# Attention values with the probabilities moving: v beside 64 columns of ones as the stationary side, gates in turned form, a new order of steps

## The chip, the cores and the metric

One Trainium2 chip, one of its cores. The metric is device time in microseconds (us). The kernel before takes 269.6 us (median of 3 runs, 269.55 to 269.61). A change of less than 0.2% can't be told from none with this kernel.

## What is computed

Two layers on x (256 positions by 1024 channels, float32), each with an RMS norm ahead of it, a residual add behind it, and a final RMS norm. The part that matters here, cut from the reference:

```python
z = hn @ w_in                                    # even: 1024 x 3584, odd: 1024 x 4096
u, v, g_a, q, k, vv, g_b = jnp.split(z, cuts)    # even layer
y_a = chunked_gmlp(u, v, ...) * silu(g_a)        # 4 groups of 128 channels, chunks of 128
y_b = moba_attention(q, k, vv) * silu(g_b)       # 8 heads of 64; one block of 256: causal softmax
h = h + concat([y_a, y_b]) @ w_out
q, k, v, g = jnp.split(hn @ w_in, 4)             # odd layer, 16 heads of 64
y = dilated_mixture(q, k, v)                     # three windows merged by their denominators
h = h + (y * silu(g)) @ w_out
```

With 256 positions both attentions are an ordinary causal softmax under one additive mask: for each head scores, exp, row sums, and y = (P v) / rowsum. SiLU is taken as g/2 times (1 + tanh(g/2)).

## The kernel before

**Products.** Every weight matrix is multiplied in three parts, so that float32 precision comes out of a cheaper form: w is split into `w_hi` (rounded to fp32r by ACT, L605) and `w_lo` (the rest, a subtraction on DVE, L743), and the activations into `hnT_hi`/`hnT_lo` or `yT_hi`/`yT_lo`; a product is hi·hi + lo·hi + hi·lo. The weights stream through `w_raw` (3 slots of 4 x 128 rows by 512 columns, loaded by SyncE) and are split by quarter (2 x 128 rows) into 9 slots.

An output of 512 columns is a *group*; a group takes two of four PSUM banks (`pair(group)`). A group consists of *items* (a quarter of weights each), an item of two half-items, and a half-item is what PE does between two other steps. There are two forms. In the **plain** form (values, gMLP inputs, gates, output projections; L1003 to L1005) 128 positions are the stationary side and 512 weight columns move: two tiles x three parts = 6 matmuls in a half-item (3 where it is for one tile: output projections and odd values). In the **turned** form (queries and keys; L962, L964, L966) 128 weight columns are stationary and 256 positions move: 12 matmuls in a half-item, and the result has channels on partitions.

**Attention of a head.** PE: `scores` (L1022, L1023) into a score bank. DVE: mask, scale and row minimum (L876). ACT: exp, with the row sums in `den` by `accum_out` (L655). PE: `transpose` (3 turns, L914) of the probabilities. ACT: copy to `probsT` (L663). For a pair of heads PE then does `values`: turned probabilities stationary (128 x 128), 64 columns of v moving, three float32 matmuls a head (L1045 to L1047), each of which is two records of the trace. DVE: reciprocal of four row sums and one multiply into `y` (L883, L885). The y of 8 heads is multiplied by its gate (`gating`, L859, L863), and every 256 channels of y are turned by PE again (`y_pair`, 4 turns, L914), rounded by ACT (L667) and split by DVE (L893) for the output projection.

**Order.** `steps()` writes one list that every engine walks, doing its own part of each step and waiting on semaphores. The list is the product half-items in order, with the other steps put in by tables: `HEADS_AT` (for each set of 8 heads the half-items at which values, transposes and scores stand), `EVEN_AT`, `NORM_AT`, `ODD_AT`, `END_AT`; `LAST_ROUND` bounds how far the splits of weights run ahead. Engines are in-order: what is written later in the list waits behind what is written earlier on the same engine. In the even layer the groups are vv, k, q, v, gb (gate of the attention), u, ga, then the output projection; in the odd layer two tiles of v, q, k, q, k, two gates, and the output projection. A product waits on `lo_ready` for its quarter, an output product also on `y_lo`; a `values` step waits on `attended` of the pair before it, since there is one `value_bank`. Below, "half-item n" counts product half-items from the start, 0 to 199: gb is 32 to 39, u 40 to 47, ga 48 to 55, the even output projection starts at 56, the second odd q is 136 to 143, the odd gates 152 to 167, the odd output projection starts at 168.

## Time and profile before

| | |
|---|---|
| median of 3 runs | 269.6 us |
| the profiled execution, its own time | 269.5 us |
| its span, first to last instruction | 267.7 us |
| PE busy (matmul) | 259.2 us, 97% |
| PE weight loads, beside the matmuls | 230.9 us, 86% |
| DVE busy | 179.2 us, 67% |
| ACT busy | 158.7 us, 59% |
| POOL busy | 24.2 us, 9% |
| mean granted TensorE clock | 0.994 |

The duration of one matmul in the trace is from its start to the modelled end of its results, and the next one begins long before that: the cost of a matmul in a stream is the distance from its start to the next start, not its duration. The same holds to a smaller degree for DVE and ACT, where a start follows the one before by some 0.06 to 0.09 us less than its duration. Where rows are merged ("x3") the second column is the time from the first start to the last end.

### The profile page before, as it was taken

To read this page: it belongs to the slowest core of one execution; us is meant where nothing else is said; L and a number is where in the kernel's file an instruction comes from. 1 tells how busy PE (TensorE), PEld (TensorE's weight loads), DVE (VectorE), ACT (ScalarE), POOL (GpSimd) and SP (SyncE) were. 2 spreads that over 40 slices of the span, in tenths; PEclk is the share of its full clock that TensorE was granted. 3 is DMA by queue.
4 is the path that set the end of the run, shared out by engine and by line. 5 is a ranking of instruction groups with operands and counts; after the bars stand their busy time and mean duration, and the time that the engine had idled before them with its cause. 6 is when DMAs were issued, how large, how long until landed. Compare 5 with 4: busy or idle time off the path is not lost.

```text
span 267.7 us, 4264 instructions
## 1 busy us (share of the span) xinstructions
PE 259.2 (97%) x1598; PEld 230.9 (86%) x1598; DVE 179.2 (67%) x327; ACT 158.7 (59%) x301; POOL 24.2 (9%) x52
## 2 busy tenths in 40 slices
PE   7999999999999999999999999999999999999990
PEld 7889998888888888887888999999998888988880
DVE  2976999648997986757677337575756758522643
ACT  5866857684856853556467464678657675640232
POOL 3016320001100000010000000300003001000021
PEclk9999999999999999999999999999999999999997
DMA  7999839504089654544539923563341542000004
GB/s 237 395 392 382 276 108 338 183 11 157 5 294 331 188 190 129 177 146 160 172 124 369 306 87 122 194 183 133 126 150 41 157 160 69 12 0 0 2 1 157
DMA packets 22452, 44.59 MB, mean 167 GB/s; under 512 B 1056, under 2 KB 1312, under 8 KB 22432
## 3 DMA queue, kind: packets, MB, share of 16 engines
q1 hardware_dynamic: 21712, 43.00, 46.9%
q10 hardware_dynamic: 576, 0.79, 0.8%
q0 software_dynamic: 144, 0.52, 0.6%
q8 instruction: 13, 0.21, 0.3%
q14 instruction: 7, 0.06, 0.1%
HBM read 43.26 MB, written 1.05 MB: 166 GB/s over the span
## 4 chain that ended last, share of the span: by engine, by line
PE 89%; DVE 4%; ACT 2%; issue 1%; DMA 1%; POOLq 0%; POOL 0%; DVEq 0%; ACTq 0%
PE products L1003 16%; PE products L1005 16%; PE products L1004 16%; PE products L962 8%; PE products L966 8%; PE products L964 8%; PE turned L914 4%; PE products L984 3%; DVE k_low L789 2%; PE attended L1047 2%; PE attended L1046 2%; PE scores L1022 2%; PE scores L1023 2%; DVE w_lo L743 2%; PE attended L1045 2%
## 5 line engine op out<-in xcount | busy, mean ns | idle before, releaser
L743 DVE TENSOR_TENSOR w_lo<-w_raw,w_hi 128x1024 fp32r<-128x1024 f32 x74 | 89.0, 1226 | 8.8 <-ACT w_hi L605 8.0
L605 ACT CAST w_hi<-w_raw 128x1024 fp32r<-128x1024 f32 x74 | 76.1, 1048 | 28.6 <-PE products L1005 9.6
L962 PE MATMUL products<-hnT_hi,w_hi 128*128 128x256 f32 x192 | 54.8, 285 | 0.0
L966 PE MATMUL products<-hnT_hi,w_lo 128*128 128x256 f32 x192 | 54.3, 283 | 0.0
L964 PE MATMUL products<-hnT_lo,w_hi 128*128 128x256 f32 x192 | 54.3, 283 | 0.0
L1003 PE MATMUL products<-w_hi,hnT_hi 128*128 128x512 f32 x128 | 51.4, 402 | 0.1
L1005 PE MATMUL products<-w_lo,hnT_hi 128*128 128x512 f32 x128 | 50.1, 391 | 0.0
L1004 PE MATMUL products<-w_hi,hnT_lo 128*128 128x512 f32 x128 | 50.0, 391 | 0.0
L962 PEld LDWEIGHTS products<-hnT_hi,w_hi 128*128 128x128 f32 x192 | 36.8, 191 | 0.5 <-DVE w_lo L743 0.4
L964 PEld LDWEIGHTS products<-hnT_lo,w_hi 128*128 128x128 f32 x192 | 36.8, 192 | 0.0
L966 PEld LDWEIGHTS products<-hnT_hi,w_lo 128*128 128x128 f32 x192 | 36.8, 191 | 0.0
L655 ACT ACTIVATE probs<-probs,least 128x128 f32<-128x128 f32 (+1 forms) x48 | 21.4, 447 | 22.7 <-DVE least L876 22.7
L1005 PEld LDWEIGHTS products<-w_lo,hnT_hi 128*128 128x128 f32 x128 | 24.0, 188 | 5.3
L1003 PEld LDWEIGHTS products<-w_hi,hnT_hi 128*128 128x128 f32 x128 | 24.1, 188 | 4.5 <-issue 0.5
L1004 PEld LDWEIGHTS products<-w_hi,hnT_lo 128*128 128x128 f32 x128 | 24.1, 188 | 4.0
L1003 PE MATMUL products<-w_hi,yT_hi 128*128 128x512 f32 x64 | 25.6, 400 | 0.0
L1005 PE MATMUL products<-w_lo,yT_hi 128*128 128x512 f32 x64 | 25.0, 391 | 0.0
L1004 PE MATMUL products<-w_hi,yT_lo 128*128 128x512 f32 x64 | 24.9, 390 | 0.0
L663 ACT COPY probsT<-turned 128x384 f32<-128x384 f32 x24 | 11.4, 474 | 5.4 <-PE turned L914 5.3
L1005 PEld LDWEIGHTS products<-w_lo,yT_hi 128*128 128x128 f32 x64 | 12.0, 188 | 2.6
L560 ACT ACTIVATE tanh<-h 128x512 f32<-128x512 f32 x8 | 5.1, 632 | 15.4 <-DVE h L901 15.3
L1004 PEld LDWEIGHTS products<-w_hi,yT_lo 128*128 128x128 f32 x64 | 12.0, 188 | 2.3
(144 smaller groups left out, 360.5 us busy)
## 6 DMA issues: line engine op xcount, KB each, us to landing
w_raw<-in_c_w_in SPq DMA_DIRECT2D x16, 1024.0 KB, 5.5
w_raw<-in_ab_w_in SPq DMA_DIRECT2D x12, 1024.0 KB, 6.3
w_raw<-in_ab_w_out SPq DMA_DIRECT2D x4, 1024.0 KB, 5.2
w_raw<-in_c_w_out SPq DMA_DIRECT2D x4, 1024.0 KB, 5.1
w_raw<-in_ab_w_in SPq DMA_DIRECT2D x4, 256.0 KB, 4.4
w_raw<-in_ab_w_in SPq DMA_DIRECT2D x2, 512.0 KB, 7.5
h<-in_x SPq DMA_DIRECT2D x2, 512.0 KB, 11.2
out<-hn SPq DMA_DIRECT2D x4, 256.0 KB, 2.2
```

The lines of the kernel that those rows point to most:

```text
L605: nc.scalar.copy(w_hi[:, n % SPLIT_SLOTS, :, :], w_raw[:, half % RAW_SLOTS, part, :]).then_inc(hi_ready, 1)
L655: last = nc.scalar.activation(probs[:, n % 2, a:b], probs[:, n % 2, a:b], ACT.Exp, scale=-1.0, bias=least[:, n, t:t + 1], accum_out=den[:, ...
L663: nc.scalar.copy(probsT[:, n % 2, :], turn_bank[:, 0:3 * P]).then_inc(probsT_ready, 1)
L743: nc.vector.tensor_tensor(w_lo[:, n % SPLIT_SLOTS, :, :], w_raw[:, half % RAW_SLOTS, part, :], w_hi[:, n % SPLIT_SLOTS, :, :].bitcast(fp32 ...
L914: return nc.tensor.matmul(to, of, ident[:], is_transpose=True, start=True, stop=True)
L962: nc.tensor.matmul(to, wh, hi[:, chunk, :], start=begins and c % 2 == 0, stop=False, skip_group_check=True)
L964: nc.tensor.matmul(to, wh, lo[:, chunk, :], start=False, stop=False, skip_group_check=True)
L966: last = nc.tensor.matmul(to, wl, hi[:, chunk, :], start=False, stop=ends, skip_group_check=True)
L984: nc.tensor.matmul(to[:], x_part[:, chunk, t * P:(t + 1) * P], w_hi[:, slot, half_item, :], start=begins and x_part is hi, stop=False)
L1003: nc.tensor.matmul(to[:], xh, w_hi[:, slot, half_item, :], start=begins, stop=False)
L1004: nc.tensor.matmul(to[:], xl, w_hi[:, slot, half_item, :], start=False, stop=False)
L1005: last = nc.tensor.matmul(to[:], xh, w_lo[:, slot, half_item, :], start=False, stop=ends)
```

## The change

1. **Values.** v is kept as blocks of 192 columns for each pair of heads: head a, 64 columns of ones, head b (`v`, and for the second odd half `hn`). A head's stationary side is 128 columns of that (`value_and_ones`), v and ones in one order or the other, and the turned probabilities move: 256 columns against the first 128 keys, 128 columns against the last 128. Both results of a pair fill `value_bank`: for each head 64 partitions of turned y and 64 partitions that all hold the row sums. So exp has no `accum_out` any more, and DVE takes reciprocals of 64 x 256 numbers twice and multiplies 64 x 256 twice for a pair of heads. `y` of the attention is now turned from the start.
2. **Gates** gb and both odd gates take the turned form of product (kind `gate_turned`). The even one is scaled by `rstd_rows` on DVE before its tanh (two 128 x 512 operations more).
3. **No turn by PE** for six of the eight `y_pair` steps; the two of gMLP (2 and 3) keep it.
4. Buffers: `probs` has 3 slots instead of 2; `ones` lies in `probsT`; the layer-norm gain and bias lie in `gate` and are loaded after weight half 8, behind a wait on `mask_built`; POOL fills in the ones (two memsets).
5. **Order.** All tables of the order are new.

```diff
-LAST_ROUND = {2: 6, 3: 7, 4: 9, 5: 9, 6: 9, 7: 9, 8: 11, 9: 13, 10: 14, 11: 15, 12: 15, 13: 17, 14: 18, 15: 19, 16: 20,
...
+LAST_ROUND = {2: 6, 3: 8, 4: 9, 5: 10, 6: 7, 7: 11, 8: 12, 9: 13, 10: 15, 11: 17, 12: 15, 13: 19, 14: 17, 15: 17, 16: 21, 17: 22,
...
-    ((10, 14, 19, 23),
+    ((9, 16, 22, 25),
...
-    whole("even_in", gb, "gate", 1)
+    whole("even_in", gb, "gate_turned", 1)
...
-        whole("odd_in", 3 * D + c * BLOCK, "gate", c)
+        whole("odd_in", 3 * D + c * BLOCK, "gate_turned", c)
...
+                if n == LN_AFTER:
+                    sp.wait_ge(mask_built, 2)
+                    sp.dma_start(ln_g, gmlp_ln_g.partition_broadcast(P)).then_inc(ln_loaded, 16)
...
+        def value_and_ones(head, t):
+            pair_of_set = head // 2 % HALF_CHUNKS
+            store = v_in_hn[t] if head >= EVEN_HEADS + HEADS_OF_SET else v[:, t]
+            return store[:, pair_of_set, (head % 2) * HEAD:(head % 2 + 2) * HEAD]
...
 # ACT, scores
-                        last = nc.scalar.activation(probs[:, n % 2, a:b], probs[:, n % 2, a:b], ACT.Exp,
-                                                    scale=-1.0, bias=least[:, n, t:t + 1],
-                                                    accum_out=den[:, n, t:t + 1])
+                        last = nc.scalar.activation(probs[:, n % 3, a:b], probs[:, n % 3, a:b], ACT.Exp,
+                                                    scale=-1.0, bias=least[:, n % 4, t:t + 1])
...
 # DVE, values
-                    chain(nc.vector.reciprocal(rden[:, pair_of, :], den[:, pair_of, :]), inverted, n + 1)
-                    column = value_column(2 * n) + (BLOCK if n < EVEN_HEADS // 2 else 0)
-                    nc.vector.tensor_tensor(
-                        y[:, :, column:column + 2 * HEAD].rearrange("p t (a d) -> p a t d", a=2),
-                        value_bank[:, 0:4 * HEAD].rearrange("p (a t d) -> p a t d", a=2, t=TILES),
-                        rden[:, pair_of, :].unsqueeze(3).to_broadcast([P, 2, TILES, HEAD]),
-                        ALU.mult).then_inc(attended, 1)
+                    for a in range(2):
+                        last = nc.vector.reciprocal(sums[rows_of(a), :],
+                                                    value_bank[rows_of(1 - a), a * SEQ:(a + 1) * SEQ])
+                    chain(last, inverted, n + 1)
+                    for a in range(2):
+                        last = nc.vector.tensor_tensor(turned_y(n)[rows_of(a)],
+                                                       value_bank[rows_of(a), a * SEQ:(a + 1) * SEQ],
+                                                       sums[rows_of(a), :], ALU.mult)
+                    last.then_inc(attended, 1)
...
 # DVE, evacuate of an even gate_turned (the odd ones only have the second loop)
+                        for i, bank in enumerate(pair(n)):
+                            nc.vector.tensor_tensor(
+                                gate[:, place, i, :].rearrange("p (a b) -> p a b", b=SEQ),
+                                bank[:].rearrange("p (a b) -> p a b", b=SEQ),
+                                rstd_rows[:].unsqueeze(1).to_broadcast([P, 2, SEQ]), ALU.mult).then_inc(gate_scaled, 1)
...
 # PE, values
-                        nc.tensor.matmul(first, pT[:, 0:P], v0, start=True, stop=True)
-                        nc.tensor.matmul(second, pT[:, P:2 * P], v0, start=True, stop=False)
-                        last = nc.tensor.matmul(second, pT[:, 2 * P:3 * P], v1, start=False, stop=True)
+                        nc.tensor.matmul(value_bank[:, cols], value_and_ones(2 * n + a, 0), probsT[:, a, 0:SEQ],
+                                         start=a == 0, stop=False, skip_group_check=True)
+                        last = nc.tensor.matmul(value_bank[:, cols][:, P:], value_and_ones(2 * n + a, 1),
+                                                probsT[:, a, SEQ:3 * P], start=False, stop=a == 1,
+                                                skip_group_check=True)
```

**Where the order matters, first place: DVE in the even layer**, from the evacuation of the gate gb (half-item 40) to the multiplication by it. `w_lo` is the split of a quarter of weights; the rows before, of the kernel before:

```order
L796 SCALAR_TENSOR_TENSOR gate<-tanh,products 128x512 [waits tanh_ready] x2
L743 TENSOR_TENSOR w_lo<-w_raw,w_hi 128x1024 [waits hi_ready] x2
...
L743 TENSOR_TENSOR w_lo<-w_raw,w_hi 128x1024 [waits hi_ready]
L883 RECIPROCAL rden<-den 128x4 [waits values_done]
L885 TENSOR_TENSOR y<-attended,rden 128x2x2x64 [waits inverted]
L743 TENSOR_TENSOR w_lo<-w_raw,w_hi 128x1024 [waits hi_ready] x4
L883 RECIPROCAL rden<-den 128x4 [waits values_done]
L885 TENSOR_TENSOR y<-attended,rden 128x2x2x64 [waits inverted]
L743 TENSOR_TENSOR w_lo<-w_raw,w_hi 128x1024 [waits hi_ready] x2
L859 SCALAR_TENSOR_TENSOR y<-y,half_rstd,gate 128x512 [waits dve_emptied,attended] x2
```

The same place of the changed kernel:

```order
L851 SCALAR_TENSOR_TENSOR gate<-tanh,gate 128x512 [waits tanh_ready,gate_scaled]
L851 SCALAR_TENSOR_TENSOR gate<-tanh,gate 128x512 [waits tanh_ready]
L789 TENSOR_TENSOR w_lo<-w_raw,w_hi 128x1024 [waits hi_ready]
L940 RECIPROCAL sums<-attended 64x256 [waits values_done]
L940 RECIPROCAL sums<-attended 64x256
L944 TENSOR_TENSOR y<-attended,sums 64x256 [waits inverted]
L944 TENSOR_TENSOR y<-attended,sums 64x256
L789 TENSOR_TENSOR w_lo<-w_raw,w_hi 128x1024 [waits hi_ready] x3
...
L789 TENSOR_TENSOR w_lo<-w_raw,w_hi 128x1024 [waits hi_ready] x2
L940 RECIPROCAL sums<-attended 64x256 [waits values_done]
...
L789 TENSOR_TENSOR w_lo<-w_raw,w_hi 128x1024 [waits hi_ready] x3
L940 RECIPROCAL sums<-attended 64x256 [waits values_done]
```

Three `values` steps of DVE (pairs 1, 2 and 3) now stand behind the evacuation of gb, before it was two (2 and 3), and each has four operations of 256 columns.

**Second place: PE at a `values` step** in the odd attention; the kernel before:

```order
L1045 MATMUL attended<-v,probsT 128x64 [waits y_lo,attended,probsT_ready]
L1046 MATMUL attended<-v,probsT 128x64
L1047 MATMUL attended<-v,probsT 128x64
L1045 MATMUL attended<-v,probsT 128x64
L1046 MATMUL attended<-v,probsT 128x64
L1047 MATMUL attended<-v,probsT 128x64
```

and the change:

```order
L1103 MATMUL attended<-probsT,hn 128x256 [waits y_lo,attended,probsT_ready]
L1105 MATMUL attended<-probsT,hn 128x128
L1103 MATMUL attended<-probsT,hn 128x256
L1105 MATMUL attended<-probsT,hn 128x128
```

Six matmuls of 64 moving columns became two of 256 and two of 128.

**Third place: DVE at the end of the odd attention**, from the evacuation of the last gate to the last split of y; the kernel before:

```order
L796 SCALAR_TENSOR_TENSOR gate<-tanh,products 128x512 [waits tanh_ready] x2
L883 RECIPROCAL rden<-den 128x4 [waits values_done]
L885 TENSOR_TENSOR y<-attended,rden 128x2x2x64 [waits inverted]
L863 TENSOR_TENSOR y<-y,gate 128x512 [waits dve_emptied,attended] x2
L893 TENSOR_TENSOR yT_lo<-attended,yT_hi 128x512 [waits y_hi]
L893 TENSOR_TENSOR yT_lo<-turned,yT_hi 128x512 [waits y_hi]
```

and the change:

```order
L851 SCALAR_TENSOR_TENSOR gate<-tanh,products 128x512 [waits tanh_ready] x2
L940 RECIPROCAL sums<-attended 64x256 [waits values_done]
L940 RECIPROCAL sums<-attended 64x256
L944 TENSOR_TENSOR y<-attended,sums 64x256 [waits inverted]
L944 TENSOR_TENSOR y<-attended,sums 64x256
L940 RECIPROCAL sums<-attended 64x256 [waits values_done]
...
L920 TENSOR_TENSOR y<-y,gate 128x512 [waits dve_emptied,attended] x2
L952 TENSOR_TENSOR yT_lo<-y,yT_hi 128x512 [waits y_hi]
L789 TENSOR_TENSOR w_lo<-w_raw,w_hi 128x1024 [waits hi_ready]
L952 TENSOR_TENSOR yT_lo<-y,yT_hi 128x512 [waits y_hi]
```

Two pairs (10 and 11) now stand between the last gate and the gating, before it was one, and one split of weights stands between the two splits of y. On PE the last two values steps stand at half-items 169 and 176 (before: 166 and 173).

## Rows read from the trace of the kernel before

**Rows 1.** Windows: length, busy us (instructions) by engine, PEclk, DMA share, GB/s
```profile
5.00:22.00 17.00, 16.50 (x94) 14.19 (x93) 14.80 (x28) 13.62 (x22) 3.07 (x7) 1.00 1.05 391
22.00:98.50 76.50, 76.50 (x475) 67.96 (x474) 63.62 (x110) 51.16 (x91) 8.29 (x11) 1.00 0.59 200
...
172.50:200.00 27.50, 27.32 (x235) 27.12 (x235) 18.31 (x49) 18.86 (x49) 0.04 (x1) 1.00 0.40 132
200.00:241.60 41.60, 41.37 (x255) 36.30 (x254) 24.72 (x62) 25.22 (x60) 3.25 (x5) 1.00 0.24 78
```

**Rows 2.** Timeline, PE: plain form at half-item 58, turned form at half-item 144
```profile
99.82 0.39 PE L1005 MATMUL products<-w_lo,yT_hi 128*128 128x512 f32 x1
100.05 0.39 PE L1003 MATMUL products<-w_hi,yT_hi 128*128 128x512 f32 x1
...
182.76 0.28 PE L966 MATMUL products<-hnT_hi,w_lo 128*128 128x256 f32 x1
182.88 0.28 PE L962 MATMUL products<-hnT_hi,w_hi 128*128 128x256 f32 x1
```

**Rows 3.** Timeline, PE: two y_pair steps between products
```profile
93.72 0.60 PE L914 MATMUL attended<-ident,y 128*128 128x128 f32 x4
...
94.51 0.48 PE L1003 MATMUL products<-w_hi,hnT_hi 128*128 128x512 f32 x1
94.82 0.40 PE L1004 MATMUL products<-w_hi,hnT_lo 128*128 128x512 f32 x1
```

**Rows 4.** Timeline, PE: a values step (its first records), and a mix step
```profile
65.56 0.33 PE L1045 MATMUL attended<-v,probsT 128*128 128x64 f32 x2
...
66.84 0.50 PE L914 MATMUL turned<-ident,probs 128*128 128x128 f32 x3
...
77.89 1.05 PE L1055 MATMUL scores<-hn 128*128 128x128 f32 x8
78.69 0.48 PE L1003 MATMUL products<-w_hi,hnT_hi 128*128 128x512 f32 x1
```

**Rows 5.** Groups of DVE by form: count, busy us, mean ns, idle before
```profile
L743 DVE TENSOR_TENSOR w_lo<-w_raw,w_hi 128x1024 fp32r<-128x1024 f32 x74 | 89.0, 1226 | 8.8 <-ACT w_hi L605 8.0
L748 DVE TENSOR_TENSOR w_lo<-w_raw,w_hi 128x512 fp32r<-128x512 f32 x4 | 2.8, 692 | 0.1
L885 DVE TENSOR_TENSOR y<-attended,rden 128x256 f32<-128x256 f32 x12 | 5.1, 425 | 0.4
L876 DVE CUSTOM_DVE_ANT_0 probs<-scores,mask_even 128x128 f32<-128x128 f32 x8 | 2.3, 287 | 1.5 <-PE turned L914 1.5
```

**Rows 6.** All reciprocals: duration ns min/median/max
```profile
L883 DVE RECIPROCAL rden<-den x12: 171/176/179, 61.5 to 241.9; 128x4 f32<-128x4 f32 x12
```

**Rows 7.** Timeline, DVE: a values step of the kernel before
```profile
77.78 0.17 DVE L883 RECIPROCAL rden<-den 128x4 f32<-128x4 f32 x1
77.99 0.42 DVE L885 TENSOR_TENSOR y<-attended,rden 128x256 f32<-128x256 f32 x1
78.33 1.22 DVE L743 TENSOR_TENSOR w_lo<-w_raw,w_hi 128x1024 fp32r<-128x1024 f32 x1
```

**Rows 8.** Windows, columns as in rows 1: DVE's two stretches
```profile
72.60:96.30 23.70, 23.70 (x133) 20.40 (x132) 21.73 (x35) 15.84 (x25) 0.00 (x0) 1.00 0.78 266
184.40:226.40 42.00, 41.77 (x298) 38.67 (x297) 28.83 (x75) 28.20 (x69) 3.25 (x5) 1.00 0.31 103
```

**Rows 9.** Timeline, PE: last product of gb, and values of pair 10
```profile
69.73 0.39 PE L1005 MATMUL products<-w_lo,hnT_hi 128*128 128x512 f32 x1
...
231.29 0.33 PE L1045 MATMUL attended<-v,probsT 128*128 128x64 f32 x2
```

**Rows 10.** Timeline, DVE: evacuations of gb and of the second odd q; last gating
```profile
72.63 1.27 DVE L796 SCALAR_TENSOR_TENSOR gate<-tanh,products 128x512 f32<-128x512 f32 x2
...
184.41 2.81 DVE L789 TENSOR_TENSOR q_own<-products,q_own 64x512 fp32r<-64x512 f32 x4 [2.12 <-ACT q_own L617]
...
242.55 1.29 DVE L863 TENSOR_TENSOR y<-y,gate 128x512 f32<-128x512 f32 x2
```

More of the change, by code:

```diff
@@ L65 @@
+    (27, ("mix_u", 0)), (28, ("y_pair", 1)), (28, ("mix_u", 1)), (29, ("mix", 1)), (36, ("gating", 1)),
+    (42, ("y_pair", 2)), (43, ("y_pair", 3)),
 )
 NORM_AT = (
-    (-13, ("residual", 0, 0)), (-10, ("residual", 0, 1)), (-6, ("scale", 0)), (-3, ("hidden", 0)),
-    (-2, ("residual", 1, 0)), (4, ("residual", 1, 1)), (5, ("scale", 1)), (12, ("hidden", 1)),
+    (-18, ("residual", 0, 0)), (-13, ("residual", 0, 1)), (-5, ("scale", 0)), (-3, ("hidden", 0)),
+    (-3, ("residual", 1, 0)), (4, ("residual", 1, 1)), (13, ("scale", 1)), (13, ("hidden", 1)),
@@ L69 @@
 )
 ODD_AT = (
-    (1, ("gating", 2)), (4, ("y_pair", 4)), (7, ("y_pair", 5)), (19, ("gating", 3)), (21, ("y_pair", 6)),
-    (22, ("y_pair", 7)),
+    (0, ("gating", 2)), (3, ("y_pair", 4)), (3, ("y_pair", 5)), (20, ("gating", 3)), (22, ("y_pair", 6)),
+    (26, ("y_pair", 7)),
 )
@@ L278, in build @@
         tanh = sb("tanh", [P, TILES, BLOCK])
-        probs = sb("probs", [P, 2, 3 * P])
+        probs = sb("probs", [P, 3, 3 * P])
         probsT = sb("probsT", [P, 2, 3 * P])
-        least = sb("least", [P, N_HEADS, 2])
-        den = sb("den", [P, N_HEADS, 2])
-        rden = sb("rden", [P, N_HEADS, 2])
+        sums = sb("sums", [P, SEQ])
+        least = sb("least", [P, 4, 2])
         mask_even = sb("mask_even", [P, 2 * P])
@@ L791, in _ @@
                         last.then_inc(heads_low, 1)
+                elif what == "evacuate" and GROUPS_OF_BANKS[n][0] == "gate_turned":
+                    place = GROUPS_OF_BANKS[n][1]
+                    if n < FIRST_ODD:
+                        dve.wait_ge(products_done, LAST_ITEM_OF_GROUP[n] + 1)
+                        for i, bank in enumerate(pair(n)):
+                            nc.vector.tensor_tensor(
+                                gate[:, place, i, :].rearrange("p (a b) -> p a b", b=SEQ),
+                                bank[:].rearrange("p (a b) -> p a b", b=SEQ),
+                                rstd_rows[:].unsqueeze(1).to_broadcast([P, 2, SEQ]), ALU.mult).then_inc(gate_scaled, 1)
+                        dve.wait_ge(gate_scaled, 2)
+                    for i, bank in enumerate(pair(n)):
+                        dve.wait_ge(tanh_ready, tanh_writes_before(n) + i + 1)
+                        last = nc.vector.scalar_tensor_tensor(
+                            out=gate[:, place, i, :], in0=tanh[:, i, :], scalar=1.0,
+                            in1=gate[:, place, i, :] if n < FIRST_ODD else bank[:], op0=ALU.add, op1=ALU.mult)
+                    last.then_inc(dve_emptied, 1)
                 elif what == "evacuate" and GROUPS_OF_BANKS[n][0] == "gate":
@@ L924, in _ @@
             for _ in range(WARM):
[L925 removed]
+                nc.tensor.matmul(value_bank[:, 0:P], ones, ones, start=True, stop=True)
             started = set()
@@ L1030, in _ @@
                     for i in range(3):
-                        last = turn(turn_bank[:, i * P:(i + 1) * P], probs[:, n % 2, i * P:(i + 1) * P])
+                        last = turn(turn_bank[:, i * P:(i + 1) * P], probs[:, n % 3, i * P:(i + 1) * P])
                     last.then_inc(probs_turned, 1)
@@ L1057, in _ @@
                     last.then_inc(mix_done, 1)
-                elif what == "y_pair":
+                elif what == "y_pair" and n in GMLP_PAIRS:
                     chunk, bank = y_place(n)
-                    pe.wait_ge(gated, n // 2 + 1)
-                    same_bank = [i for i in range(n) if y_place(i)[1] is bank]
-                    if same_bank:
-                        pe.wait_ge(y_lo, same_bank[-1] + 1)
+                    pe.wait_ge(gated, 2)
                     if bank is value_bank:
```

130 lines of the change are left out of this document (76 added, 54 removed).

## The prediction

> **What bounds the kernel now.** I read the windows first [rows 1]: from 5 us to the last matmul PE is busy in all but 0.9 us of the stretches shown (17.00 - 16.50, and 0.18, 0.23 in the last two), always at the upper of its two clock levels, 2.4 GHz (PEclk 1.00). So every instruction that leaves PE is worth its distance to the next start, as long as no other engine becomes late. DVE comes next: 63.6 of 76.5 us in the stretch with the even attention, 43 of 69 us in the two with the odd one. The timeline of PE gives the distances [rows 2 to 4], the groups and the timeline of DVE the prices there [rows 5 to 7], and two windows how much DVE has to do where the change puts more on it [rows 8].
>
> **PE's own sum.** Turns of y: two neighbouring y_pair steps take 93.72 to 94.51 = 0.79 us, and the product behind them starts its successor 0.31 instead of 0.23 us later: 0.87 us for two [rows 3]. Six steps go, the first two as such a pair, the four others one by one at about 0.44 us: -2.63 us. Gates: 3 groups x 48 = 144 matmuls of 512 columns at 0.227 us become 288 of 256 columns at 0.120 us [rows 2]: 144 x (0.240 - 0.227) = +1.87 us. Values: before, 12 records of 64 columns from 65.56 to 66.84, 1.28 us [rows 4]. The change has 4 records of 256 columns and 4 of 128. A record of 128 float32 columns costs no more than one of 64: 8 of them from 77.89 to 78.69, the last overlapped, 0.11 us each. No row shows 256. The ends are 0.11 (no dearer) and 0.22 (twice 128 columns), so 0.9 to 1.33 us a step; I take 1.33, since from 256 to 512 columns the products go from 0.120 to 0.227 us, so columns count there. 12 x 0.05 = +0.6 us, at the other end 12 x -0.38 = -4.6 us. PE's sum: -2.63 + 1.87 + 0.6 = -0.2 us, nothing that could be measured.
>
> The Trainium skill (TensorE: Matmul & The Clock Gate, Part 1) puts a warm matmul at N/2.4 ns plus 2.5 ns, so the gates would cost 144 x 2.5 = 0.36 us instead of 1.87. The trace has 13 ns over the columns, not 2.5 [rows 2], so I keep 1.87; by the page the sum would be 1.5 us lower.
>
> **DVE's step.** A values step took 0.55 us (77.78 to 78.33) [rows 7]. Now it is two reciprocals of 256 columns and two multiplications. A multiplication of this size is 0.34 us to the next start, and 0.42 where something waits for it [rows 5, 7]; 64 partitions I take as dear as 128. The reciprocal decides. Only one of 4 columns is shown: median 176 ns [rows 6]. Other operations have 1226 and 692 ns for 1024 and 512 columns, 1.04 ns a column and 159 ns fixed; 128 columns at 287 leave 154. A reciprocal at that pace would take 159 + 4 = 163 ns. It takes 13 ns more. If all over 159 is its columns, (176 - 159)/4 = 4.2 ns a column; if the first column is in a fixed part of 156, between the two, (176 - 156)/3 = 6.7. The lower end is 1.04 ns (0.42 us for 256, with 13 ns of another cause), the upper the slowest row, (179 - 156)/3 = 7.7 ns, 2.1 us. I take 5.5 ns, the middle of the two readings: 158 + 256 x 5.5 = 1.57 us. The step is then 2 x 1.57 + 0.05 + 0.34 + 0.42 = **3.9 us instead of 0.55**, 12 times 3.4 = 40 us more for DVE. At the lower end it is 1.4 us, at the upper 5.0.
>
> The Trainium skill (VectorE: DVE Perf Modes, "First, the fixed hardware budget") speaks against the change here: the reciprocal is an iterative divide with a repeat count of 8. Eight of the trace's 1.04 ns would be 8.3 ns a column, 2.3 us for 256, an estimate from that page and rows 5, and the total would come out near 291. The trace has 17 to 20 ns over the fixed part for four columns [rows 5, 6], which is less than 8.3 each, but well over 1.04.
>
> **Place A, even attention.** In the changed kernel DVE can't begin the evacuation of gb before PE's last product of it, which starts at 69.73: 70.1 us [rows 9]. Two new scalings at the pace of the two evacuations (1.27 us) and 0.1 us for the tanh behind the second: 71.5. From the first evacuation, 72.63, to the end of y_lo of pair 1, 96.3, DVE now has 21.73 us of work [rows 8, 10], and the same steps stand there after the change, but for pair 1 of the values, which came in: 21.7 - 2 x 0.55 + 3 x 3.9 = 32.3, so y_lo is ready at 103.8. PE wants it at half-item 58, before at 100.05 [rows 2]: less 0.87 for the turns, plus one values step of 1.33 and 2 x 0.05, 100.6. **+3.2 us** at least. With the reciprocal at 0.42 us DVE is ready at 96.3 and the place costs nothing; at 2.1 us it is 6.5.
>
> **Place B, odd attention.** DVE evacuates the second odd q from 184.41 [rows 10] and is through with pair 9 at 226.4, with 28.83 us of work in it [rows 8]. Changed: six values steps, + 6 x 3.35 = 20.1; two splits of y (2 x 0.62) and one of weights (1.2) now stand ahead of pair 9, + 2.4. 51.3 us of work: ready at 235.7 without any idle time. PE wants it for pair 10. Before, it went from 182.88 to 231.29 [rows 2, 9]; now two half-items of 1.44 and one of 0.68 more stand ahead of it, 14 gate half-items are 0.08 longer each, 6 values steps 0.05, and a turn of y (0.44) and 0.4 us of waits go: 182.9 + 48.4 + 2.9 + 0.7 + 1.1 + 0.3 - 0.8 = 235.5. So +0.2 with no idle time; but DVE idled 13 us of these 42 for PE and ACT [rows 8], and I leave 2 us of that: **+2.2 us**. Reciprocal fast: nothing (DVE 15 us early); slow: +8.8.
>
> **Place C, the end of the odd attention.** From the start of values of pair 10 PE has 1.6 us of it and the turn, 7 half-items of 0.68 and a turn to values of pair 11, done at +8.1, and wants y_lo of y_pair 6 eight half-items later, at +13.5. DVE from +8.1: 3.9 us, gating 1.3 [rows 10], ACT's rounding 0.6 (estimated by DVE's, it overlaps), y_lo 0.7: +14.6, and the split of weights between the two y_lo puts the second 0.5 us later still: **+1.6 us**. Fast: none; slow: +2.7.
>
> **What costs nothing.** ACT loses 48 reads of row sums; it waits for DVE in the attention, so this only helps. POOL does 3 us of work in the 17 us from 5 to 22 us, and the first memset comes on top there [rows 1]; should it delay `mask_built`, SP's loads of the layer-norm vectors and the weight half behind them wait with it, 1 us at most, and the slots cover that. If `mix` 1, which now stands behind the evacuation of u on DVE, is late, DVE stands still until PE reaches it; then comes 5 us of work before y_lo of pair 1, against 5.5 us of PE's: 0.5 us of room, and only if DVE isn't late anyway.
>
> **Sum.** The profiled execution took 269.5, the median is 269.6. 269.5 - 0.2 + 3.2 + 2.2 + 1.6 = 276.3; queues at scores and transposes, which stand only 2 to 3 half-items behind each other now, I put at +0.7: **277 us**.
>
> **Rivals.**
> 1. *The reciprocal is no slower than other operations* (0.42 us), its 13 ns come from elsewhere. Then the three places cost nothing, and the sum is PE's: 269.3 us, a wash. For it: one short row can't tell a pace; the new order stretches nothing in the places that I read. Against: other short distances fit 159 ns well. Chance 0.14.
> 2. *Faster*: rival 1, and in the `values` step of PE a record costs what its weight load costs, whatever it moves. 64 and 128 columns both at 0.11 us speak for it [rows 4]. It decides from below 0.2 us for a record of 256 columns: 12 x 4 x 0.02 = 1 us less than my price, that is 268.3 us; at 0.11 it is 269.5 - 0.76 - 4.6 = 264.1. It needs DVE in time. Against: products of 512 columns cost nearly twice those of 256. Chance 0.10.
> 3. *DVE far over*: the reciprocal at its upper end. 269.5 - 0.2 + 6.5 + 8.8 + 2.7 + 0.7 = 288 us. PE would also stand still longer in one piece, so its clock could fall to 1.2 GHz for a while. Chance 0.08.
> 4. *It isn't the step that it says*: the order takes away PE's waits only. There is 0.9 us of them [rows 1], so 268.4 at best; held in rival 2's chance.
>
> **How the numbers follow.** The forecast, reciprocals at 4 to 7 ns a column and 274 to 283 us, has 0.68; rival 3 0.08, rival 1 0.14, rival 2 0.10. Faster by over 0.2%: 0.10 + 0.01 = 0.11. Within 0.2%: 0.11, most of rival 1. Slower: 0.68 + 0.08 + 0.02 of rival 1 (new waits) = 0.78. 0.2% is about what can be told from no change. The range leaves out rivals 2 and 3 and takes in the wash: 268.8 to 285; the likeliest case alone is 274 to 283.
>
> **What would show it.** Each reciprocal 1.2 to 1.8 us; DVE busy some 220 us instead of 179, PE with idle time of 6 to 8 us ended by DVE (y_lo, attended, w_lo, or probs behind `least`), the larger part in the even attention between u and the output projection; records of 256 columns 0.22 us apart; products of the gates 0.12 us apart. A reciprocal under 0.7 us makes the forecast wrong from its root, since at that price place A is just met. If it is right and the time is still below 272, the order has hidden more of DVE's work than my sums allow.

## The result, and the profile after

The changed kernel takes **291.7 us** (median of 4 runs, 290.7 to 292.7), the kernel before in the same session 269.6: 1.081 times as long, 95% interval 1.079 to 1.084. The forecast of "slower" held; 277 us and the range up to 285 did not. The change costs 22.1 us, not 7.4. Where runs of one kernel lie over 1.5% above its fastest (two of the four of e6, at 288.55 and 288.65, its profiled execution among them), the time given is that of the other runs.

The page of the changed kernel (line engine op, what it writes and reads, count | busy us, mean ns | idle before):

```profile
span 290.3 us, 4385 instructions
## 1 busy us (share of the span) xinstructions
PE 265.9 (92%) x1670; PEld 238.5 (82%) x1670; DVE 225.2 (78%) x353; ACT 154.1 (53%) x253; POOL 26.5 (9%) x54
...
PE   8999999998977988999999999999898898888791
...
DVE  3887998498899999579386274949999977977644
...
PEclk9999999999997999999999999999999999799799
...
PE 42%; DVE 35%; DMA 9%; issue 6%; ACT 5%; SPq 1%; POOL 1%; POOLq 0%; DVEq 0%; ACTq 0%
...
L940 DVE RECIPROCAL sums<-attended 64x256 f32<-64x256 f32 x24 | 42.1, 1754 | 2.6 <-PE attended L1105 2.2
L697 ACT ACTIVATE probs<-probs,least 128x128 f32<-128x128 f32 (+1 forms) x48 | 18.6, 447 | 41.0 <-DVE least L933 41.0
```

PE is busy 265.9 us instead of 259.2 and DVE 225.2 instead of 179.2. A reciprocal takes 1754 ns where 176 were spent on four columns [rows 6]. Of the slices 10 to 16 (some 65 to 116 us) five show PE at 7 or 8 tenths, and in the last third most do; three times PEclk is down with them. In the chain, DVE has 35%. The waits (engine, line <- who ended them: us in total, times, longest):

```profile
ACT probs L697 <- DVE least L933: 41.0, 13, 6.5
...
PE turned L973 <- ACT probsT L704: 4.6, 2, 2.5
...
PE scores L1081 <- DVE least L933: 3.7, 3, 1.3
...
PE products L1062 <- DVE yT_lo L952: 3.5, 3, 1.8
```

The first line is the one to read. It is no wait of PE. ACT's exp waits 41 us for `least`, which DVE's mask step writes; with copies in place of the reciprocals (e1) it is 20.4 us, 3.9 at the longest, and costs nothing: it isn't the sum that counts, but whether PE comes to wait for it. PE then waits at a turn for ACT's copy to `probsT` of the head before (L704), which stands behind that exp on ACT, or at scores for the bank that the mask empties.

The windows, after (columns as in rows 1):

```profile
74.00:90.00 16.00, 13.54 (x64) 10.93 (x63) 15.55 (x19) 7.89 (x12) 0.00 (x0) 0.92 0.33 117
90.00:110.00 20.00, 17.55 (x84) 14.00 (x83) 19.78 (x28) 11.62 (x16) 0.00 (x0) 0.98 0.51 170
183.00:205.00 22.00, 20.89 (x173) 20.39 (x171) 17.76 (x39) 12.23 (x24) 0.00 (x0) 1.00 0.45 144
205.00:232.00 27.00, 24.75 (x195) 23.98 (x196) 26.19 (x46) 14.72 (x27) 2.44 (x4) 1.00 0.26 80
232.00:255.00 23.00, 20.82 (x151) 20.09 (x150) 19.58 (x34) 10.88 (x22) 0.81 (x1) 0.93 0.18 68
255.00:284.00 29.00, 25.27 (x107) 19.88 (x105) 18.78 (x25) 6.65 (x15) 1.42 (x4) 0.94 0.00 1
```

and the same with copies in place of the reciprocals, from the first experiment below:

```profile
74.00:90.00 16.00, 15.98 (x83) 13.12 (x83) 15.71 (x25) 10.11 (x14) 0.00 (x0) 1.00 0.58 199
90.00:110.00 20.00, 20.00 (x99) 16.73 (x98) 18.67 (x31) 12.45 (x18) 0.00 (x0) 1.00 0.55 176
183.00:205.00 22.00, 22.00 (x179) 21.68 (x179) 15.56 (x36) 14.68 (x26) 2.37 (x4) 1.00 0.33 117
205.00:232.00 27.00, 27.00 (x222) 26.68 (x221) 22.13 (x56) 16.14 (x31) 0.87 (x2) 1.00 0.31 99
```

DVE was at 15.71 of 16 and 18.67 of 20 us there without any reciprocal; with them it is full for 36 us on end, and PE loses 4.9 us in them. In 205 to 232 us DVE has 26.19 of 27.

One such stop, from DVE's timeline, then ACT's, then PE's:

```profile
76.66 1.22 DVE L789 TENSOR_TENSOR w_lo<-w_raw,w_hi 128x1024 fp32r<-128x1024 f32 x1
77.91 3.52 DVE L940 RECIPROCAL sums<-attended 64x256 f32<-64x256 f32 x2
81.47 0.86 DVE L944 TENSOR_TENSOR y<-attended,sums 64x256 f32<-64x256 f32 x2
82.36 3.50 DVE L789 TENSOR_TENSOR w_lo<-w_raw,w_hi 128x1024 fp32r<-128x1024 f32 x3
85.88 0.29 DVE L933 CUSTOM_DVE_ANT_0 probs<-scores,mask_even 128x128 f32<-128x128 f32 x1
```

```profile
86.56 0.80 ACT L697 ACTIVATE probs<-probs,least 128x128 f32<-128x128 f32 x2 [6.54 <-DVE least L933]
87.27 0.45 ACT L704 COPY probsT<-turned 128x384 f32<-128x384 f32 x1
```

```profile
87.87 0.87 PE L973 MATMUL turned<-ident,probs 128*128 128x128 f32 x3 [2.46 <-ACT probsT L704]
...
88.96 0.63 PE L1063 MATMUL products<-w_hi,hnT_lo 128*128 128x512 f32 x1
...
93.39 0.67 PE L1103 MATMUL attended<-probsT,v 128*128 128x256 f32 x2 [0.81 <-DVE y L944]
```

The mask of head 7 begins at 85.88. Ahead of it on DVE stand a values step of 4.45 us (77.91 to 82.36) and three splits of weights, 3.5 us. ACT has waited 6.54 us for it, PE 2.46. What ended PE's wait was the copy at 87.27, of head 6, behind the exp of head 7. After the stop the clock is down: products of 512 columns start 0.43 us apart instead of 0.227 (88.96, then 89.39 and 89.82), the pace of 1.2 GHz instead of 2.4, until 90.67. Then `values` waits for the pair before it.

### The profile page after: what moved, and what is told of

Read it like the earlier page. It is cut to its first block, busy times and chain, and to the rows that moved or that the text cites. A ratio compares the mean times of both kernels' runs of the same rounds, so it can differ in the third digit from the quotient of the medians.

```text
span 290.3 us, 4385 instructions
## 1 busy us (share of the span) xinstructions
PE 265.9 (92%) x1670; PEld 238.5 (82%) x1670; DVE 225.2 (78%) x353; ACT 154.1 (53%) x253; POOL 26.5 (9%) x54
## 4 chain that ended last, share of the span: by engine, by line
PE 42%; DVE 35%; DMA 9%; issue 6%; ACT 5%; SPq 1%; POOL 1%; POOLq 0%; DVEq 0%; ACTq 0%
DVE sums L940 11%; DVE w_lo L789 10%; PE products L1062 8%; PE products L1063 7%; PE products L1064 7%; DMA w_raw<-in_ab_w_in 7%; PE products L1021 5%; PE products L1023 5%; PE products L1025 5%; DVE k_low L835 2%; DMA w_raw<-in_ab_w_out 2%; DVE probs L933 2%; DVE y L944 2%; ACT w_hi L641 1%; PE scores L1081 1%
## 5 line engine op out<-in xcount | busy, mean ns | idle before, releaser
L1021 PE MATMUL products<-hnT_hi,w_hi 128*128 128x256 f32 x288 | 83.2, 289 | 0.0
L1023 PE MATMUL products<-hnT_lo,w_hi 128*128 128x256 f32 x288 | 81.9, 285 | 0.0
L1025 PE MATMUL products<-hnT_hi,w_lo 128*128 128x256 f32 x288 | 81.9, 284 | 0.0
L1021 PEld LDWEIGHTS products<-hnT_hi,w_hi 128*128 128x128 f32 x288 | 55.7, 194 | 0.1
L1023 PEld LDWEIGHTS products<-hnT_lo,w_hi 128*128 128x128 f32 x288 | 55.7, 193 | 0.1
L1025 PEld LDWEIGHTS products<-hnT_hi,w_lo 128*128 128x128 f32 x288 | 55.6, 193 | 0.0
L940 DVE RECIPROCAL sums<-attended 64x256 f32<-64x256 f32 x24 | 42.1, 1754 | 2.6 <-PE attended L1105 2.2
L1062 PE MATMUL products<-w_hi,hnT_hi 128*128 128x512 f32 x80 | 32.7, 409 | 0.4 <-DVE hnT_lo L777 0.3
L1063 PE MATMUL products<-w_hi,hnT_lo 128*128 128x512 f32 x80 | 31.7, 396 | 0.0
L1064 PE MATMUL products<-w_lo,hnT_hi 128*128 128x512 f32 x80 | 31.6, 395 | 0.0
L704 ACT COPY probsT<-turned 128x384 f32<-128x384 f32 x24 | 11.3, 472 | 13.6 <-PE attended L1105 7.2
L973 PE MATMUL turned<-ident,probs 128*128 128x128 f32 x72 | 12.4, 282 | 5.7 <-ACT probsT L704 4.6
```

Of the source, the lines that this page charges most:

```text
L704: nc.scalar.copy(probsT[:, n % 2, :], turn_bank[:, 0:3 * P]).then_inc(probsT_ready, 1)
L940: last = nc.vector.reciprocal(sums[rows_of(a), :], value_bank[rows_of(1 - a), a * SEQ:(a + 1) * SEQ])
L973: return nc.tensor.matmul(to, of, ident[:], is_transpose=True, start=True, stop=True)
L1021: nc.tensor.matmul(to, wh, hi[:, chunk, :], start=begins and c % 2 == 0, stop=False, skip_group_check=True)
L1023: nc.tensor.matmul(to, wh, lo[:, chunk, :], start=False, stop=False, skip_group_check=True)
L1025: last = nc.tensor.matmul(to, wl, hi[:, chunk, :], start=False, stop=ends, skip_group_check=True)
```

## Experiments

**e1: the reciprocal alone.** The changed kernel with `tensor_copy` for `reciprocal`, so y is multiplied by the row sums instead of divided.

```diff
-    last = nc.vector.reciprocal(sums[rows_of(a), :],
+    last = nc.vector.tensor_copy(sums[rows_of(a), :],
```

> The changed kernel, each of the 24 reciprocals of 64 x 256 replaced by a copy of the same size (so y isn't divided by the row sums). Theory (the reciprocal's 1.75 us each is the whole loss): the copies take about 0.42 us, DVE has 32 us less to do, PE's waits go back to the 1 to 2 us of the kernel before, and the time is PE's own sum, 269.3 us, between 268.5 and 271. Rival (the new order, or the form of the change, makes waits of its own): well over 272, with PE still waiting at the turns and scores.

269.44 us, ratio 0.997 (0.995 to 0.9996).

```profile
span 267.3 us, 4385 instructions
## 1 busy us (share of the span) xinstructions
PE 258.3 (97%) x1670; PEld 234.7 (88%) x1670; DVE 193.3 (72%) x353; ACT 154.9 (58%) x253; POOL 26.5 (10%) x54
```

The copies take 421 ns each, so DVE has 31.9 us less to do. All of the 22 us hang on the pace of this one instruction. Products, values with ones, turns and order together come out level, as the -0.2 us of PE's own sum had it. Since this is the same program instruction by instruction, it serves as the scale for the rest: the same PE instruction can be looked up in both timelines.

| PE instruction | copies, starts | after, starts | later by |
|---|---|---|---|
| scores of head 6 | 64.54 | 66.52 | 2.0 |
| turn of head 7 | 83.22 | 87.87 | 4.6 |
| values 3 | 86.39 | 93.39 | 7.0 |
| output product that needs y_lo of pair 1 (half-item 58) | 100.55 | 109.59 | 9.0 |
| first scores of the odd attention | 173.77 | 182.91 | 9.1 |
| turn of head 21 | 231.82 | 247.62 | 15.8 |
| values 10 | 236.17 | 253.53 | 17.4 |
| output product that needs y_lo of y_pair 6 (half-item 184) | 249.77 | 271.06 | 21.3 |
| last matmul | 260.43 | 283.42 | 23.0 |

**e2: is it the clock?** Eight idle matmuls are put at four of the stops (turns of heads 7 and 21, values 11, the first half-item of item 92, which is half-item 184), meant to keep PE at work through them.

```diff
-    pe.wait_ge(probs_ready, n + 1)
     if n >= 1:
         pe.wait_ge(probsT_ready, n)
+    if n in (7, 21):
+        fill(8)     # 8 x matmul(turn_bank[:, 0:P], ident, ident)
+    pe.wait_ge(probs_ready, n + 1)
```

> The changed kernel with 8 spare float32 matmuls of 128 columns (some 1.8 us of work on PE, result unused) ahead of the waits at its four longest stops: the turn of head 7, the turn of head 21, the values of pair 11 and the first product of half-item 184. Theory (each of the three stretches at 1.2 GHz, 3.4 us long, costs PE about 1.7 us that it doesn't get back): the clock stays up there and the time falls by 3 to 5 us, to 287 to 289. Rival (PE is waiting for DVE anyway, so a slower clock in between costs nothing): no gain, 291 to 293.

291.6 us, ratio 1.081 (1.076 to 1.086): no gain. But the edit does only part of what it was meant to. At the two turns the idle matmuls stand behind `wait_ge(probsT_ready, n)`, and that is the wait at which PE stood:

```profile
87.47 2.05 PE L984 MATMUL turned<-ident 128*128 128x128 f32 x16 [2.36 <-ACT probsT L704]
89.36 0.49 PE L973 MATMUL turned<-ident,probs 128*128 128x128 f32 x3
```

They began when the stop was over and put the turn of head 7 from 87.87 to 89.36, that of head 21 from 247.62 to 250.80. At values 11 there was no stop left to fill, since PE came later by then, and they cost 1.5 us (263.75 instead of 262.21). Only those at half-item 184 covered a wait. The profile has one fall of the clock left, near 247 us.

Two things can be read from it. Values 3 began at 93.09 in spite of the 1.9 us of idle matmuls, 0.3 us sooner than in the changed kernel, for it waits for DVE's y; there PE has room, and the lower clock before it costs nothing. So the 2.4 us by which the table's rows "turn of head 7" and "values 3" differ are not the clock's own. At the end it is otherwise: the 48 products from half-item 184 on take 11.1 us here at the full clock (272.53 to 283.66) and 12.4 in the changed kernel, where it falls. This gain of 1.2 us and the 1.5 us of idle matmuls cancel. The four runs say the same: 290.7 and 290.9 us at a mean granted clock of 0.998 and 0.997, 292.3 and 293.3 at 0.990 and 0.985. The clock is worth some 1 to 2 us of the 22 (an estimate from these numbers), not the bulk.

**e3: one mask earlier.** `HEADS_AT` has scores 7 at 15 instead of 18.

```diff
-(3, 3, 5, 5, 12, 13, 13, 18)
+(3, 3, 5, 5, 12, 13, 13, 15)
```

> The changed kernel with one number of the order changed: scores of head 7 at 15 instead of 18 half-items, so that on DVE its mask stands ahead of the evacuation of the gate and of the values step of pair 1 and three splits of weights. Theory (the loss is made by masks that queue behind 4.4 us values steps, not by the sum of DVE's work): the wait of 2.6 us before the turn of head 7 goes, and the clock's fall there with it, 3 to 4 us in all, 288 us. Rival (DVE is full in this stretch, what isn't lost at the turn is lost at y_lo of pair 0 and 1 or at the weights): less than 1 us gained, 291 us, with longer waits at the even output projection.

291.09 us, 1.079 (1.075 to 1.083), not clear of the changed kernel's 290.7 to 292.7. The wait at the turn of head 7 is gone and values 3 waits instead, 4.1 us, until 93.07 instead of 93.39. In that stretch it is DVE's amount of work that decides, and its order only says at which instruction PE stands.

**e4: the same load in the kernel before.** 24 reciprocals of 64 x 256 whose results are not used, two in each values step.

```diff
+    for a in range(2):
+        nc.vector.reciprocal(spare[rows_of(a), :], value_bank[rows_of(1 - a), 0:SEQ])
```

> The kernel before with two reciprocals of 64 x 256 from the values' bank into spare memory added to every values step of DVE (24 in all, the result unused); nothing else of the change. Theory (42 us more of DVE's time in front of masks is what costs, in any form and order): 285 to 293 us. Rival (the form of the change makes DVE's work critical, the order before would hide it): under 280 us.

297.3 us, 1.102 (1.096 to 1.108). The line of them:

```profile
L887 DVE RECIPROCAL spare<-attended 64x256 f32<-64x256 f32 x24 | 42.1, 1754 | 0.6
```

The price is the same 1754 ns in another place. Here 42.1 us of added work cost 27.5 us, 0.65 for each; in the changed kernel reciprocals instead of copies are 31.9 us more work and cost 22.2, 0.70 for each. So neither the forms of the change nor its order make this work much dearer than it is elsewhere.

**e5 and e6: the division elsewhere.** Row sums come from `accum_out` again, and `probs` is scaled by their inverse before the turn, on DVE (e5) or on POOL (e6, inverse by a power of -1); DVE then only copies y out.

```diff
 # e5, DVE, at a transpose step (e6: the same two kinds of operation on POOL)
+    dve.wait_ge(probs_ready, n + 1)
+    chain(nc.vector.reciprocal(rden[:, n % 4, :], den[:, n % 4, :]), inverse, n + 1)
+    for t, (a, b) in enumerate(((0, P), (P, 3 * P))):
+        last = nc.vector.tensor_scalar(probs[:, n % 3, a:b], probs[:, n % 3, a:b],
+                                       rden[:, n % 4, t:t + 1], None, ALU.mult)
```

> The changed kernel with the division moved ahead of the turn: exp gives its row sums again (accum_out, 2 x 0.19 us on ACT a head), DVE takes the reciprocal of 128 x 2 (0.2 us) and scales the head's probabilities in place (128 x 128 and 128 x 256 in SBUF, some 0.5 us), the turn waits for that, and the values step only copies 2 x 64 x 256 (0.8 us). The result is the reference's. Theory (what counts is how much DVE does in the attention): 2.2 us a pair instead of 4.4, DVE busy some 200 us, time 269 to 273 us. Rival (the longer way from mask to turn, exp to DVE to PE, stops PE as the long reciprocals did): 275 us or more, with PE waiting at turns.

> As the run with the scaling on DVE, but the reciprocal (power -1 of 128 x 2, some 0.7 us) and the scaling of the probabilities are on POOL, which is idle for 260 us. The result is the reference's. DVE has 0.8 us a pair, nearly as before the change. Theory: DVE is out of the way, POOL's 2 us a head fit between heads that are 4 us and more apart: 268.8 to 271 us, level with the kernel before, as PE's own sum is -0.2 us. Rival (POOL's latency of over 2 us per head stands in the chain from scores to turn, which has 2 to 3 half-items of room): 273 us or more, PE waits at turns on POOL.

e5 takes 318.6 us, 1.178 (1.173 to 1.183), though DVE has 26 us less to do than after (199.1 busy). The reason stands in its timeline and waits:

```profile
200.96 2.81 DVE L838 TENSOR_TENSOR q_own<-products,q_own 64x512 fp32r<-64x512 f32 x4 [2.11 <-ACT q_own L655]
203.80 1.23 DVE L792 TENSOR_TENSOR w_lo<-w_raw,w_hi 128x1024 fp32r<-128x1024 f32 x1
204.95 0.16 DVE L942 RECIPROCAL rden<-den 128x2 f32<-128x2 f32 x1
205.14 0.55 DVE L944 TENSOR_SCALAR probs<-probs,rden 128x128 f32<-128x128 f32 x2
```

```profile
PE turned L978 <- DVE probs L944: 33.5, 16, 4.7
```

The evacuation of q waits 2.11 us for ACT, a split follows, and only then comes the scaling of a head; PE stood 4.7 us for it until 205.74. Every head now needs DVE twice in its chain (mask, then scaling), and DVE's queue holds other waits between.

e6 takes 284.2 us (283.4 and 285.1), 1.051 (1.045 to 1.056), the best form that still divides every head by its own sums. In the profiled execution PE waits 10.8 us at turns for POOL. POOL at an undisturbed head and at the worst one:

```profile
200.64 0.71 POOL L553 TENSOR_TENSOR rden<-den,minus_one 128x2 f32<-128x2 f32 x1 [3.36 <-ACT probs L718]
201.45 1.52 POOL L557 TENSOR_SCALAR probs<-probs,rden 128x128 f32<-128x128 f32 x2
```

```profile
90.37 1.73 POOL L553 TENSOR_TENSOR rden<-den,minus_one 128x2 f32<-128x2 f32 x1 [10.81 <-ACT probs L718]
92.20 3.44 POOL L557 TENSOR_SCALAR probs<-probs,rden 128x128 f32<-128x128 f32 x2
```

2.3 us a head is what POOL takes (0.71, then 1.52 for both tiles), at some heads more than the distance that the order leaves between exp and turn; at 90.37 the same three instructions took 5.3 us, and PE's turn came at 95.70. DVE was busy for 4.4 of the 5.4 us there (90.3 to 95.7), with splits above all, and for 0.65 of 2.4 at the undisturbed head; whether that stretched them was not tested.

**e7 and e8: PE's two largest terms, alone, in the kernel before.** e7: the three gates take the turned form of product, with everything else as before. e8: the six y_pair steps that the change drops don't turn y; ACT and DVE read y itself. In both the layout of a tile no longer fits what reads it, so the values are others.

```diff
 # e7
-    if kind in ("query", "key"):
+    if kind in ("query", "key") or (kind == "gate" and group != 6):
 # e8
-    elif what == "y_pair":
+    elif what == "y_pair" and n in (2, 3):
```

> The kernel before with only the products of gb and of the two odd gates in turned form, 288 matmuls of 256 columns in place of 144 of 512; what follows reads them as before, so the gates' values are wrong. Theory (13 ns more for each pair, PE alone): +1.9 us, 271.4 to 271.7. Rival (by 2.5 ns a matmul instead of 13): +0.4 us, 270.0.

> The kernel before without the turns of y by PE in six of the eight y_pair steps: ACT and DVE read y itself (so the output products get y in the wrong layout). Theory: 24 turns and six switches less on PE, -2.6 us, 266.9 to 267.4. Rival (the products wait for y_lo then): less than 1 us gained.

e7: 270.83 us, 1.0022 (1.0003 to 1.0042), +0.9 us. In the trace a turn of y behind all three gates comes at 248.47 instead of 247.22, +1.25. My 1.87 took 0.227 us for a plain product; the last one ahead of another kind of step takes up to 0.31, and the 144 removed ones average 0.234. e8: 266.94 us, 0.987 (0.984 to 0.990), -2.9 us against -2.63 in the sum. Both terms have the right sign. The turns have the right size too; the gates cost half to two thirds of what I had put, and the interval (+0.1 to +1.1 us) also holds the +0.4 of the rival, against which only the trace's +1.25 speaks.

**e9 and e10: the two attentions apart.** Reciprocals in one, copies in the other.

```diff
+    take = nc.vector.reciprocal if n < EVEN_HEADS // 2 else nc.vector.tensor_copy   # e10: >=
```

> The changed kernel with real reciprocals for the four even pairs only; for the eight odd pairs a copy of the same shape stands in their place, so the odd y is multiplied by its row sums instead of divided. Theory (the loss has separate places): PE of the changed kernel was 10.1 us late when it came to the scores of the first odd head, and with copies nothing is lost behind it: 269.4 + 10 = 279.5 us. Rival (what the even part is late by is partly won back in the odd one, where weights and splits have run ahead meanwhile): 275 us or less.

> The other half: copies in the four even pairs, real reciprocals in the eight odd ones. Theory (separate places): 7.9 us to values of pair 10 and 4.1 us behind it, 269.4 + 12 = 281.4 us, and with the run of even reciprocals the two losses add up to the 22.2 us of the whole. Rival (coupled): the odd part loses less when the even one is not late, and the two add up to under 19 us.

e9: 277.76 us, 1.030 (1.029 to 1.032). e10: 282.5 us, 1.048 (1.046 to 1.050). That is +8.3 and +13.1 over e1; together 21.4 of the 22.2. The theory's 279.5 and 281.4 were off by 1.7 and 1.1 in opposite directions, but the losses are separate places and add up. Four pairs cost 2.1 us each in the even attention, eight cost 1.6 each in the odd one.

**e11: at the price that I had taken.** From the second pair on the reciprocals take 224 columns.

```diff
+    to = SEQ if n == 0 else 224
-    last = nc.vector.reciprocal(sums[rows_of(a), :], value_bank[rows_of(1 - a), a * SEQ:(a + 1) * SEQ])
+    last = nc.vector.reciprocal(sums[rows_of(a), 0:to], value_bank[rows_of(1 - a), a * SEQ:a * SEQ + to])
```

> The changed kernel, but from the second pair on the reciprocals take 224 of the 256 columns: at 6.3 ns a column 1.55 us each, the price that the prediction had (1.57). The last 32 columns of each head are divided by the first pair's sums, so the output is not the reference's. Theory (the miss is in how DVE's work stands in the order, not in the price): DVE sheds 23 x 0.2 = 4.6 us, and what was lost falls by no more than that: 287 to 289 us. Rival (the price was the miss; beyond some load each tenth of a microsecond costs much more): 277 to 281 us.

286.95 us, 1.0645 (1.063 to 1.066). Its groups of DVE:

```profile
L941 DVE RECIPROCAL sums<-attended 64x224 f32<-64x224 f32 x22 | 34.2, 1554 | 2.2 <-PE attended L1106 1.9
...
L941 DVE RECIPROCAL sums<-attended 64x256 f32<-64x256 f32 x2 | 3.5, 1755 | 0.4 <-PE attended L1106 0.4
```

32 columns are 200 ns, 6.25 ns each, on a fixed 154. With the reciprocal at 1.554 us, just under the 1.57 of the prediction, the loss over e1 is still 17.5 us, not 7.5. So of the 14.7 us by which 277 was missed, at most 4.7 belong to the price and 10 or more to the rest, that is to where DVE's work stands and what follows from it. DVE shed 22 x 0.2 = 4.4 us of work and the kernel 4.7, but 1.2 of these are the clock: the last 48 products ran at the full clock in e11's profile, in 11.2 us instead of 12.4. In this range a microsecond of reciprocal is 0.8 to 1.1 us of time.

**e12: the old order.** All tables as they were, the forms changed.

> The changed kernel with all tables of the order (from LAST_ROUND to the last one) as they were before; the forms of products and values stay changed. Theory (the new order puts room around the slower values step): the old order loses as much more as the kernel before with added reciprocals did, 296 to 298 us. Rival (the order gives nothing, the difference of that run to the changed kernel came from the turns that left PE): 291 to 293 us.

296.5 us, 1.099 (1.097 to 1.101), 4.8 us more than with the new tables. Its longest stop is of another kind: values 2 waits 6.3 us, until 83.56, for ACT's copy to `probsT`, which stands behind a tanh that waited 7.0 us for DVE's scaling of the gate (L844), and that stood behind a values step. So the new order is worth nearly 5 us with slow reciprocals.

## Why the prediction was wrong in size

**Right.** Direction and mechanism: the reciprocal, put at 1.57 us, took 1.754, inside the bounds of 0.42 to 2.1. DVE's busy time was given as 220 us and is 225. PE's sum was -0.2 and e1 is level; of its two largest terms the turns were confirmed apart (e8), the gates came out at 0.9 to 1.25 us instead of 1.87 (e7), and gate products start 0.120 us apart, values records of 256 columns 0.22. Rivals 1 and 2 fall with the price of the reciprocal. Rival 3 (288 us) named the outcome best, clock falls included, but for another reason: it needed 2.1 us a reciprocal. Of the signs that I named one failed: the larger part of the loss is not in the even attention (8.3 us, e9) but in the odd one (13.1, e10).

**Price.** 5.5 ns a column were taken where e11 shows 6.25, so the step is 4.45 us instead of 3.9: 3.5 to 4.7 us of the total (e11). The reading by which the first column lies in the fixed part (6.7) was the closer one, and I averaged it away. As for the page VectorE: DVE Perf Modes of the Trainium skill ("First, the fixed hardware budget"): eight times the pace of 1.04 ns for each column would have been 2.3 us, an estimate; the trace shows 1.754, about six times that pace. The total of "near 291" that the page would have given came true with too high a price, and by the other error below.

**Place A: the start, not the length.** The sentence that failed is "70.1 us [...] Two new scalings [...]: 71.5". It lets DVE begin on gb as soon as PE is through. Of the copies' version (e1) and of after:

```profile
71.25 0.75 DVE L893 SCALAR_TENSOR_TENSOR hn<-hn,rstd,gate 128x512 f32<-128x512 f32 x1 [0.51 <-POOL rstd L566]
71.92 1.28 DVE L844 TENSOR_TENSOR gate<-products,rstd_rows 128x512 f32<-128x512 f32 x2
73.46 1.30 DVE L851 SCALAR_TENSOR_TENSOR gate<-tanh,gate 128x512 f32<-128x512 f32 x2 [0.26 <-ACT tanh L678]
...
99.26 0.68 DVE L952 TENSOR_TENSOR yT_lo<-y,yT_hi 128x512 fp32r<-128x512 f32 x1
```

```profile
70.34 0.75 DVE L893 SCALAR_TENSOR_TENSOR hn<-hn,rstd,gate 128x512 f32<-128x512 f32 x1 [0.81 <-POOL rstd L566]
71.01 0.68 DVE L885 BATCH_NORM_STATS2 moments<-hn 128x6 f32<-128x512 f32 x1
...
73.23 0.75 DVE L893 SCALAR_TENSOR_TENSOR hn<-hn,rstd,gate 128x512 f32<-128x512 f32 x1 [0.51 <-POOL rstd L566]
73.91 1.28 DVE L844 TENSOR_TENSOR gate<-products,rstd_rows 128x512 f32<-128x512 f32 x2
75.45 1.29 DVE L851 SCALAR_TENSOR_TENSOR gate<-tanh,gate 128x512 f32<-128x512 f32 x2 [0.26 <-ACT tanh L678]
...
108.76 0.68 DVE L952 TENSOR_TENSOR yT_lo<-y,yT_hi 128x512 fp32r<-128x512 f32 x1
```

Both halves of the gMLP norm (L885 to L893), with their waits for POOL's `rstd`, stand ahead of gb on DVE (in the kernel before they did too, from 62.62 to 70.95, and I left them out), so even with copies the gate's multiplication begins at 73.46, not 71.5. In after it begins at 75.45: 2.0 us more, for PE had stood at the scores of head 6, whose bank is emptied by a mask behind values step 0 (57.91 to 62.36) and the splits. From there to the end of y_lo of pair 1 (DVE's L952 at 108.76, so 109.44) are 34.0 us; I had 32.3, and 3 x 0.55 us of dearer steps make 33.9. The length was right. Late by 3.95 at the start and 1.7 by price: 3.2 became 9.0. The same error shows in e1. "With the reciprocal at 0.42 us DVE is ready at 96.3": it was ready at 99.94, 0.6 us before PE wanted it. Of these 3.6 us, 2.0 are the start and 1.1 the values steps, which take 1.78 us with copies (75.92 to 77.70) where I had 1.4. The 4.3 us of room that the place had on my sheet were not there.

**Place B.** From DVE's start on the second odd q (194.67) to the end of pair 9 (253.10) are 58.4 us, in which DVE is busy 54.07. I had 51.3 of work and 2 of idle time. 2.8 us more are work (price), 2.4 more idle, and 0.4 pass until PE, slowed by the lower clock from 247.6 to 251.3, comes to values 10: DVE waits 1.86 us for ACT's tanh at 233.73 and 1.38 for ACT's rounding of y at 245.67, and ACT is late there because it had waited for DVE's masks. "I leave 2 us of that" was the guess that failed. Of the 2.2 us came 8.2.

**Place C.** 1.6 us became 3.9 (21.3 - 17.4), and the last product block ran partly at the lower clock and took 1.7 us more than in e1. My "done at +8.1" took values 11 to be free of waits. PE stood 1.7 us ahead of it (262.21) for pair 10's y, whose reciprocals began only at 257.70 behind the evacuation of the last gate, and that had waited 1.35 us for ACT's tanh. So values 11 was done at +10.0: 1.9 us, and 0.55 for the dearer step.

**"Queues at scores and transposes, +0.7".** This, with the starting time in place A and the idle time in place B, is the step that failed. I priced only the places where PE waits for the product of the slow steps, and took masks for small change because they are short (0.28 and 0.42 us). PE stood 8.3 us at turns and scores (4.6 and 3.7 in the waits above), some of which it would otherwise have stood later. For a mask waits out whatever stands ahead of it, and a values step of 4.4 us with the splits is more than the 2 to 3 half-items between scores and turn. All stops of PE over 1 us from 183 to 250 us are at scores or turns of probabilities (204.93, 224.14, 231.47, 247.62), none at a values step itself.

**What stays open.** How much of the 10 us is idle time of DVE that another order could remove. e3 moved one mask and gained at most 0.6; e12 lost 4.8. In 74 to 110 us, with 35.3 of 36 us busy, no order of the same steps within the stretch can help much; in 183 to 205, 232 to 255 and 255 to 284 us DVE has 4.2, 3.4 and 10 us free. Nor did a version beat the kernel before: PE's sum alone is as long as before, so the best that a cheap division could give is e1's 269.4.

## What to carry to other kernels

Before a row-sum inverse is moved from a column per row (4 columns) to a form replicated over a tile (256 columns), get the per-column pace of the reciprocal on DVE: here 6.25 ns, six times that of a multiplication. When an in-order engine gets a long step, don't price only who waits for that step: list what short work stands behind it, and who waits for that; and take its starting time in a stretch from what stands ahead of it in its own queue, not from the engine that feeds it. If the time that the bounding engine's own work takes doesn't fall, the change can't win, whatever the order. And when idle work is put in to cover a stop, put it ahead of the wait that ends last there, and look in the trace whether it ran during the stop.
